# Modulation weights in stacked partition groups with selector sums, and rotary scores from stacked high and low parts

## The chip, the cores and the metric

One core of one Trainium2 chip runs the whole kernel. The metric is device time in microseconds of one execution: the kernel before takes 1735.68 us, the median of 3 runs (1734.07 to 1736.79).

## The reference

Two blocks follow each other, all in float32, for 256 tokens of width 2048. The first has two layers of latent attention, a gated short convolution and attention over a memory; the second has a Fourier mixer and a squared-ReLU MLP, both modulated by a vector `c`. What the change touches is this:

```python
# first block, for each of 2 layers l: 8 heads, 128 plain + 64 rotary dimensions
q = (rmsnorm(q_lat, q_norm_g[l]) @ w_uq[l]).reshape(b, s, 8, 192)
q = concat([q[..., :128], apply_rope(q[..., 128:], cos, sin)], axis=-1)
k_pe = apply_rope(k_pe, cos, sin)                     # one rotary key for all heads
k = concat([k_nope, broadcast_to(k_pe, (b, s, 8, 64))], axis=-1)
sc = einsum('bqhd,bkhd->bhqk', q, k) * 192 ** -0.5    # then softmax, then @ v
# second block: w_mod is 2048 x 12288 (100.7 MB), c one vector of 2048
sh1, sc1, g1, sh2, sc2, g2 = split(silu(c) @ w_mod + b_mod, 6)
h = rms_norm(x, norm_g[0]) * (1 + sc1) + sh1
x = x + g1 * rms_norm(fourier_mix(h) @ fnet_w_out, norm_g[1])
h = rms_norm(x, norm_g[2]) * (1 + sc2) + sh2
x = x + g2 * rms_norm(square(relu(h @ w_mlp_in)) @ w_mlp_out, norm_g[3])
```

## The kernel before, in words

**Steps.** The work of TensorE is cut into 576 steps, each of which multiplies half a weight unit (a unit is up to 128 x 2048 float32, 1 MB, in a ring of four, `raw`). Steps 0 to 143 are layer 0 and steps 144 to 287 layer 1 of the first block, 288 to 319 the projection of the Fourier mixer, 320 to 575 the MLP. Every weight product is made of three rounded products. ScalarE copies a half unit to its rounded high part (`split_hi`, L373 to L380) three steps ahead, VectorE subtracts for the low part (`split_lo`, L382 to L387), and TensorE multiplies high by high, high by low and low by high (`fm_half`, L398 to L409, with the weights stationary and 256 tokens moving; `tm_half`, L411 to L423, with up to 512 weight columns moving). The rounded type is `float32r`. A product of plain `float32` operands is issued as two instructions on TensorE.

**Order.** Each engine walks through the steps in a loop of its own, and at given steps does other work in its own queue's order: what stands behind a waiting instruction waits too. SyncE issues nearly all loads (L474 to L563): unit `u` when the unit four before it has been multiplied, and behind it `load_mods` (L477 to L485).

**w_mod.** The product with `silu(c)` is done on VectorE beside all the rest. The 12288 columns are taken in 12 chunks of 1024 columns. A unit is 128 rows of a chunk (512 KB, one DMA, a ring of three, `modw`), 16 units to a chunk, 192 in all; VectorE adds unit times a column of factors `cv` to `modacc` (`mod_unit`, L986 to L999, inside the step loop at L1185 and before the step's group end). `mod_plan` (L172 to L184) gives each unit a step: one of `mod_slots`, which leaves out the steps in `HEAVY`. After the 16th unit of a chunk it picks a step, at least two later, at which TensorE sums `modacc` over the partitions (`mod_sums`, L1352 to L1357: eight plain float32 products of a 128 x 128 piece of `modacc` with one column of ones into bank `M[3]`); the next chunk starts after it. TensorE waits in its order for all units of the chunk. VectorE adds the result to `modT` one step later (`mod_added`, L1001 to L1007). The sums stand at steps 49, 82, 105, 126, 166, 204, 232, 255, 277, 308, 359 and 421.

**Rotary part.** The groups `uq` (steps 40 to 47 of a layer, two steps and two heads a group) and `ukv` (steps 48 to 55) alternate between two accumulators, so a group needs the one that the group before the last used. At the end of a `uq` group ScalarE makes the half-swapped copy `swap` and the copy to `O` (L692 to L697), and VectorE makes `qpe` (L1053 to L1060). `rotary_keys` (L1086 to L1099) makes the rotated key in two zero-padded versions `kpe`, for even and odd heads. At steps 59, 62, ... 80 TensorE makes the scores of a head (L1435 to L1443): for each 128 queries one plain float32 product with `kn` and one with `kpe`.

Of the kernel before, what the change touches and what calls it, by code (L numbers as in the profile page):

```python
# [5 lines left out]
F32 = mybir.dt.float32  # L6
# [7 lines left out]
P = 128  # L14
# [124 lines left out]
MCH = MODCOLS // 1024  # L139
# [4 lines left out]
HEAVY = ({21, 24, 26, 28, 30, 31, 32, 33, 39, 40, 41, 42, 44, 46, 48, 49, 51, 52, 54, 55, 56, 63} | set(range(64, 69)) | {72, 77, 84}  # L144
# [26 lines left out]

def mod_plan():  # L172

    units, sums, free = {}, {}, -1
    for step in mod_slots():
        if len(units) == MCH * KT or step <= free:
            continue
        units[step] = len(units)
        if len(units) % KT == 0:
            free = step + 2  # L180
            while not may_sum(free):
                free += 1
            sums[free] = len(units) // KT - 1
    return units, sums  # L184
# [3 lines left out]
assert len(MOD_AT) == MCH * KT and len(MOD_SUM) == MCH  # L188
# [3 lines left out]
assert MOD_END[5] < LH + GATE_ROW[0] and MOD_END[9] < BY_TOKEN[1]  # L192
# [16 lines left out]
def build_program(nc, x, memt, positions, small, w_in, w_uq, w_ukv, w_mk, w_mv, w_o, post_g,  # L209
# [3 lines left out]
    with ctx:  # L213
# [37 lines left out]
        kpe = at("kpe", [P, 2, SEQ], A + 40)  # L251
# [30 lines left out]
        ones = at("ones", [P, 8], m + 0.5)  # L282
        gs = at("gs", [P, G_CONST], m + 0.5625)
# [16 lines left out]
        assert origin + (m + 2.34375) * 1024 <= nc.sbuf_top  # L300
# [27 lines left out]
        lat = [{n: sem(f"{w}_{n}") for n in LN} for w in ("q", "kv")]  # L328
        kpe_T, swap_in, rope_prod, rope_out, conv_step = map(sem, ("kpe_T", "swap_in", "rope_prod", "rope_out", "conv_step"))
# [11 lines left out]
        x2_xn, x2_T, x2_val, x2_hi, x2_lo = map(sem, ("x2_xn", "x2_T", "x2_val", "x2_hi", "x2_lo"))  # L341
        first_hi, first_lo, mem_first = sem("first_hi"), sem("first_lo"), sem("mem_first")
# [223 lines left out]
        def _(pool):  # L566
# [4 lines left out]
            nc.gpsimd.memset(sc[:, XP:XP + 8], EPS).then_inc(pow_set, 1)  # L571
            pool.wait_ge(pow_set, 4)
# [33 lines left out]
        def _(act):  # L606
# [65 lines left out]

            def ended(act, l, g):
# [18 lines left out]
                if name == "uq":  # L692
                    act.wait_ge(rope_out, l * 5 + i + 1)
# [4 lines left out]
                if name == "ukv":  # L698
                    nc.scalar.activation(V[:, :, 256 * i:256 * i + 256],
# [39 lines left out]
            for l in range(DEPTH):  # L739
                base = l * LH  # L740
                for s in range(LH):
# [183 lines left out]
        def _(dve):  # L925
# [60 lines left out]
            def mod_unit(at_step):  # L986

                j = MOD_AT[at_step]
                c, k = j // KT, j % KT
                dve.wait_ge(mod_in[j % MRING], 16 * (j // MRING + 1))  # L990
                co = cv[:, 2 * KT + k:2 * KT + k + 1]
                if k == 0:
# [8 lines left out]
            def mod_added(at_step):  # L1001

                if at_step - 1 in MOD_SUM:
                    c = MOD_SUM[at_step - 1]
                    dve.wait_ge(mod_T, c + 1)
                    cols = modT[:, 8 * c:8 * c + 8]
                    tt(cols, M[3][:, MODCOL:MODCOL + 8], cols, ALU.add).then_inc(mod_out, 1)  # L1007
# [78 lines left out]
            def rotary_keys(l):  # L1086

                dve.wait_ge(swap_in, 5 * l + 1)
                for e in range(2):
                    half = slice(64 * e, 64 * e + 64)  # L1090
                    nc.vector.memset(kpe[64 - 64 * e:128 - 64 * e, e, :], 0.0)
                    tt(kpe[half, e, :], M[0][half, 0:SEQ], cosT[half, :], ALU.mult)
                tt(swap[:, :], swap[:, :], sinT[:, :], ALU.mult).then_inc(rope_prod, 1)
                dve.wait_ge(rope_prod, 5 * l + 1)
                for e in range(2):
                    half = slice(64 * e, 64 * e + 64)
                    w = tt(kpe[half, e, :], kpe[half, e, :], swap[half, :], ALU.add)
                w.then_inc(rope_out, 1)
                dve.wait_ge(rope_out, 5 * l + 1)  # L1099

            for l in range(DEPTH):
                base = l * LH
                for s in range(LH):
# [100 lines left out]
                    if l == DEPTH - 1 and s == GATE_ROW[0]:  # L1204

                        dve.wait_ge(mod_out, 6)
# [46 lines left out]
            dve.wait_ge(mod_out, 10)  # L1253
# [31 lines left out]
            for q in range(4):  # L1285
                base = ML_H + 64 * q
                for s in range(65 if q < 3 else 64):
# [8 lines left out]
                    if q == 2 and s == 2:  # L1296
                        dve.wait_ge(mod_out, 12)
# [45 lines left out]
        def _(pe):  # L1343
# [8 lines left out]
            def mod_sums(at_step):  # L1352
                c = MOD_SUM[at_step]
                pe.wait_ge(mod_used, KT * (c + 1))
                for t in range(8):
                    i = mm(M[3][:, MODCOL + t:MODCOL + t + 1], modacc[:, t * P:(t + 1) * P], ones[:, 0:1], True, True)
                i.then_inc(mod_T, 1)  # L1357

            for l in range(DEPTH):
                base = l * LH  # L1360
                for s in range(LH if l + 1 < DEPTH else LH - 8):
# [60 lines left out]
                    for h in range(NH):  # L1422
# [3 lines left out]
                        if s == QK_AT[h]:  # L1426
                            if h == 0:
                                pe.wait_ge(acc_act, act_reads(l, G_OF["xin"] - 1))
                                pe.wait_ge(rope_out, l * 5 + 5)
# [151 lines left out]
            pe.wait_ge(mod_out, 10)  # L1581
# [98 lines left out]
```

## Time and profile before

| What | Value |
|---|---|
| median of 3 runs | 1735.68 us |
| the profiled execution, its own time | 1735.06 us |
| its span, first to last instruction | 1733.3 us |
| mean granted TensorE clock | 0.992 |
| TensorE busy / VectorE / ScalarE | 98% / 67% / 48% |
| bytes loaded from HBM | 404.58 MB |

Durations below come from the one profiled execution. PE is TensorE's matmuls, PEld its weight loads, DVE is VectorE, ACT ScalarE, SPq the queue of SyncE. Instructions overlap on an engine, so what one costs in a row of its like is the distance between two starts.

### The profile page before, as it was taken

How to read it: one execution, taken by the hardware profiler on the slowest of the kernel's cores; microseconds unless marked ns; L12 is line 12 of the kernel's file. 1: busy time of each engine (PE TensorE's matmuls, PEld its weight loads, DVE VectorE, ACT ScalarE, POOL GpSimd, SP SyncE). 2: the span in 40 equal slices, each digit the busy share in tenths (PEclk: the TensorE clock that was granted, in tenths of full speed). 3: DMA queues.
4: the chain of work that ended last, by engine and by line, in shares of the span. 5: the costliest groups of instructions: out<-in, count | busy, mean ns of one | idle time of the engine just before them, and what ended most of it. 6: DMA issues, size and time to landing. Idle time of an engine off the chain costs nothing.

```text
span 1733.3 us, 24590 instructions
## 1 busy us (share of the span) xinstructions
PE 1703.2 (98%) x10180; PEld 1522.9 (88%) x10180; DVE 1163.2 (67%) x1234; ACT 840.2 (48%) x1151; POOL 19.4 (1%) x34
## 2 busy tenths in 40 slices
PE   7999999999999999999999989999999999999997
PEld 7899999987889999998898878888888888888886
DVE  6777657787867767678759568776555465555555
ACT  6557445444645645544454364434443344334442
POOL 0000000000100000000000000000000000000000
PEclk9999999999999999999999989999999999999999
DMA  8688567897768857688738548788656565655663
GB/s 298 214 280 304 191 215 243 318 343 287 254 203 275 295 176 266 219 313 311 262 135 317 200 155 280 259 290 286 191 174 193 193 193 185 216 188 188 195 193 123
DMA packets 184943, 408.29 MB, mean 236 GB/s; under 512 B 8928, under 2 KB 21504, under 8 KB 184064
## 3 DMA queue, kind: packets, MB, share of 16 engines
q1 hardware_dynamic: 184336, 404.58, 68.3%
q8 instruction: 81, 1.33, 0.3%
q10 hardware_dynamic: 496, 2.14, 0.3%
q14 instruction: 30, 0.25, 0.1%
HBM read 404.58 MB, written 2.11 MB: 235 GB/s over the span
## 4 chain that ended last, share of the span: by engine, by line
PE 94%; DMA 2%; DVE 1%; issue 1%; ACT 1%; POOL 0%; DVEq 0%; SPq 0%; POOLq 0%; ACTq 0%
PE banks L390 93%; DMA modw<-in_w_mod 1%; DMA raw<-in_w_mv 1%; PE banks L1419 1%; PE banks L1382 0%; DVE modacc L998 0%; DVE wlo L386 0%; ACT whi L379 0%; DMA raw<-in_w_mk 0%; PE banks L1390 0%; DVE X L967 0%; PE banks L1575 0%; DVE xn L1179 0%; DVE otok L927 0%; ACT junk L615 0%
## 5 line engine op out<-in xcount | busy, mean ns | idle before, releaser
L386 DVE TENSOR_TENSOR wlo<-raw,whi 128x1024 fp32r<-128x1024 f32 (+3 forms) x563 | 666.4, 1189 | 449.1 <-ACT whi L379 447.7
L379 ACT ACTIVATE whi<-raw 128x1024 fp32r<-128x1024 f32 (+3 forms) x563 | 577.4, 1031 | 685.8 <-PE banks L390 657.2
L390 PE MATMUL banks<-H,whi 128*128 128x256 f32 (+1 forms) x3072 | 743.6, 325 | 1.2 <-DVE H L927 1.2
L390 PE MATMUL banks<-H,wlo 128*128 128x256 f32 x2048 | 578.1, 282 | 0.0
L390 PEld LDWEIGHTS banks<-H,whi 128*128 128x128 f32 x3072 | 515.4, 191 | 50.7 <-DVE H L927 1.6
L390 PE MATMUL banks<-whi,Y 128*128 128x512 f32 x1472 | 458.9, 391 | 1.1 <-DVE wlo L386 1.1
L390 PEld LDWEIGHTS banks<-H,wlo 128*128 128x128 f32 x2048 | 390.9, 191 | 0.1
L390 PEld LDWEIGHTS banks<-whi,Y 128*128 128x128 f32 x1472 | 277.9, 189 | 60.0 <-DVE wlo L386 1.9
L390 PE MATMUL banks<-wlo,Y 128*128 128x512 f32 x768 | 300.0, 391 | 0.0
L998 DVE SCALAR_TENSOR_TENSOR modacc<-modw,cv,modacc 128x1024 f32<-128x1024 f32 x180 | 230.1, 1279 | 17.1 <-DMA modw<-in_w_mod 17.0
L390 PEld LDWEIGHTS banks<-wlo,Y 128*128 128x128 f32 x768 | 144.9, 189 | 29.8
L390 PE MATMUL banks<-whi,H 128*128 128x512 f32 (+1 forms) x480 | 139.3, 370 | 0.0
L390 PEld LDWEIGHTS banks<-whi,H 128*128 128x128 f32 x480 | 87.7, 188 | 13.7
L390 PE MATMUL banks<-wlo,H 128*128 128x512 f32 (+1 forms) x256 | 94.5, 369 | 0.0
L390 PEld LDWEIGHTS banks<-wlo,H 128*128 128x128 f32 x256 | 48.1, 188 | 7.3
L779 ACT ACTIVATE prob<-banks,sc 128x256 f32<-128x256 f32 x48 | 22.4, 471 | 49.2 <-DVE sc L1139 49.2
L390 PE MATMUL banks<-memh,whi 128*128 128x256 f32 x128 | 38.8, 303 | 6.7 <-DVE wlo L927 6.7
L911 ACT ACTIVATE Y<-sqr 128x1024 fp32r<-128x1024 f32 x16 | 17.0, 1061 | 44.3 <-DVE sqr L1308 44.3
L390 PE MATMUL banks<-meml,whi 128*128 128x256 f32 x128 | 37.9, 296 | 0.0
L390 PE MATMUL banks<-memh,wlo 128*128 128x256 f32 x128 | 37.8, 296 | 0.0
L390 PEld LDWEIGHTS banks<-memh,whi 128*128 128x128 f32 x128 | 26.4, 206 | 7.2 <-issue 7.1
L828 ACT ACTIVATE prob<-prob,sc 128x256 f32<-128x256 f32 x48 | 21.8, 502 | 22.4 <-DVE sc L1143 22.1
(198 smaller groups left out, 1293.4 us busy)
## 6 DMA issues: line engine op xcount, KB each, us to landing
modw<-in_w_mod SPq DMA_DIRECT2D x192, 512.0 KB, 6.4
raw<-in_w_in SPq DMA_DIRECT2D x72, 1024.0 KB, 5.2
raw<-in_w_mlp_in SPq DMA_DIRECT2D x64, 1024.0 KB, 5.3
raw<-in_w_mlp_out SPq DMA_DIRECT2D x64, 1024.0 KB, 5.1
raw<-in_w_o SPq DMA_DIRECT2D x32, 1024.0 KB, 6.2
raw<-in_w_fnet SPq DMA_DIRECT2D x16, 1024.0 KB, 6.4
raw<-in_w_mv SPq DMA_DIRECT2D x8, 1024.0 KB, 6.1
raw<-in_w_mk SPq DMA_DIRECT2D x7, 1024.0 KB, 6.0
```

The lines of the kernel that those rows point to most:

```text
L379: nc.scalar.activation(hi_part(step, n), raw[u % RAW][:, (step % 2) * n:(step % 2) * n + n], ACT.Copy).then_inc(hi_ready, 1)
L386: nc.vector.tensor_tensor(wlo[u % RAW][:, part], raw[u % RAW][:, part], hi_part(step, n).bitcast(F32), ALU.subtract).then_inc(lo_ready, 1)
L390: return nc.tensor.matmul(o, a, b, start=start, stop=stop, skip_group_check=True)
L779: w = nc.scalar.activation(prob[:, b, t, :], M[b][:, t * SEQ:(t + 1) * SEQ], ACT.Exp, scale=scale, bias=sc[:, NM + 2 * b + t:NM + 2 * b + ...
L828: w = nc.scalar.activation(prob[:, b, t, :], prob[:, b, t, :], ACT.Copy, scale=sc[:, RINV + 2 * b + t:RINV + 2 * b + t + 1])
L911: nc.scalar.activation(Yhi[:, 4 * j:4 * j + 4, :], sqr[:, :, :], ACT.Copy).then_inc(m_hi, 1)
L998: nc.vector.scalar_tensor_tensor(modacc[:, :], modw[j % MRING][:, :], co, modacc[:, :], ALU.mult, ALU.add).then_inc(mod_used, 1)
L1419: i = nc.tensor.transpose(M[2][:, kt * SEQ + t * P:kt * SEQ + (t + 1) * P], prob[:, b, t, kt * P:(kt + 1) * P], ident[:, :])
```

## The change

The chunks become four passes of 64, 32, 64 and 32 units. A unit is still 512 KB in one ring slot, but its partitions are four groups of 32 (or two of 64), and each group holds the same 32 (64) rows of `w_mod` for another 1024 columns; it is loaded by four (two) DMAs. Column factors come from `cvx`, in which ScalarE repeats `cv` by groups with 20 small copies at steps 15 to 17. The sum is made of eight products with four (two) selector columns `sel`, which GpSimd sets at the start. By the planner's own rules the four sums stand at steps 125, 204, 307 and 421. Five more steps of a layer are kept free of units, and the steps freed of sums take units, so that 73, 72, 17 and 30 units stand in the two layers, the mixer and the MLP, where it was 74, 70, 17 and 31.

The rotated queries get a high part in one half of the partitions and their low part in the other (`qr`), the rotated key, which both halves hold alike, a high part `krh` and a low part `krl`. Two float32r products replace the one plain product. The key loses its two padded versions.

```diff
-MCH = MODCOLS // 1024
+MOD_PASS = ((0, 4, 0), (2 * D, 2, 64), (3 * D, 4, 96), (5 * D, 2, 160))
+MOD_UNITS = 192
-HEAVY = ({21, ..., 63} | set(range(64, 69)) | {72, 77, 84}
+HEAVY = ({21, ..., 63} | set(range(64, 69)) | {72, 77, 84, 91, 98, 119, 126, 133}
...
@@ load_mods (SyncE)
-                        k, c = j % KT, j // KT
-                        sp.dma_start(modw[j % MRING][:, :], w_mod[k * P:(k + 1) * P, 1024 * c:1024 * (c + 1)]).then_inc(mod_in[j % MRING], 16)
+                        col, groups, j0 = MOD_PASS[pass_of(j)]
+                        n, k = P // groups, (j - j0) * (P // groups)
+                        for e in range(groups):
+                            sp.dma_start(modw[j % MRING][e * n:(e + 1) * n, :],
+                                         w_mod[k:k + n, col + 1024 * e:col + 1024 * (e + 1)]).then_inc(mod_in[j % MRING], 16)
@@ GpSimd, at the start: sel[:, 0:4] and sel[:, 4:6] get ones by groups of 32 and 64 partitions (7 memsets)
@@ ScalarE
+            def rotary_hi(l, i):
+                act.wait_ge(rope_out, l * 5 + i + 1)
+                if i == 0:
+                    nc.scalar.activation(krh[:, :], kr[:, :], ACT.Copy).then_inc(rope_hi, 1)
+                else:
+                    nc.scalar.activation(qr[0:64, 2 * i - 2, :], qpe[0:64, i - 1, :], ACT.Copy)
+                    nc.scalar.activation(qr[64:128, 2 * i - 1, :], qpe[64:128, i - 1, :], ACT.Copy).then_inc(rope_hi, 1)
+            def spread_factors(part):
+                act.wait_ge(cv_step, 3)
+                for groups, c0, es in ((4, 0, (0, 1)), (4, 0, (2, 3)), (2, 64, (0, 1)))[part:part + 1]:
+                    n = P // groups
+                    for e in es:
+                        for j in range(groups):
+                            w = nc.scalar.activation(cvx[e * n:(e + 1) * n, c0 + j:c0 + groups * KT:groups],
+                                                     cv[j * n:(j + 1) * n, 2 * KT:], ACT.Copy)
+                w.then_inc(cv_ready, 1)
...
                 if name == "uq":
-                    act.wait_ge(rope_out, l * 5 + i + 1)
+                    rotary_hi(l, i)
                     for b in range(4):
...
                 if name == "ukv":
+                    if i == 0:
+                        rotary_hi(l, 4)
...
+                    if l == 0 and 15 <= s < 18:
+                        spread_factors(s - 15)
@@ VectorE
+                if j == 0:
+                    dve.wait_ge(cv_ready, 3)
...
+            def rotary_lo(l, i):
+                dve.wait_ge(rope_hi, l * 5 + i + 1)
+                if i == 0:
+                    w = tt(krl[:, :], kr[:, :], krh[:, :].bitcast(F32), ALU.subtract)
+                else:
+                    tt(qr[64:128, 2 * i - 2, :], qpe[0:64, i - 1, :], qr[0:64, 2 * i - 2, :].bitcast(F32), ALU.subtract)
+                    w = tt(qr[0:64, 2 * i - 1, :], qpe[64:128, i - 1, :], qr[64:128, 2 * i - 1, :].bitcast(F32), ALU.subtract)
+                w.then_inc(rope_lo, 1)
             def ended(l, g):
+                if name == "ukv" and i == 0:
+                    rotary_lo(l, 4)
...
                 if name == "uq":
+                    rotary_lo(l, i)
                     dve.wait_ge(swap_in, 5 * l + i + 2)
@@ rotary_keys (VectorE): two memsets and four products of 64 partitions become two of 128
@@ TensorE
-                pe.wait_ge(mod_used, KT * (c + 1))
+                groups = MOD_PASS[c][1]
+                pe.wait_ge(mod_used, MOD_LAST[c])
+                own = sel[:, 0:4] if groups == 4 else sel[:, 4:6]
                 for t in range(8):
-                    i = mm(M[3][:, MODCOL + t:MODCOL + t + 1], modacc[:, t * P:(t + 1) * P], ones[:, 0:1], True, True)
+                    i = mm(M[3][:, MODCOL + groups * t:MODCOL + groups * (t + 1)], modacc[:, t * P:(t + 1) * P], own, True, True)
...
                                     mm(o, O[:, h, tok], kn[:, h, :], True, False)
-                                    i = mm(o, qpe[:, h // 2, tok], kpe[:, h % 2, :], False, True)
+                                    mm(o, qr[:, h, tok], krh[:, :], False, False)
+                                    i = mm(o, qr[:, h, tok], krl[:, :], False, True)
```

## Rows read from the trace of the kernel before

**Rows 1.** The page: busy time of the bounding engine, and the slices.
```profile
PE 1703.2 (98%) x10180; PEld 1522.9 (88%) x10180; DVE 1163.2 (67%) x1234; ACT 840.2 (48%) x1151; POOL 19.4 (1%) x34
...
PE   7999999999999999999999989999999999999997
```

**Rows 2.** The page: shares of the chain that ended last, by line.
```profile
PE banks L390 93%; DMA modw<-in_w_mod 1%; DMA raw<-in_w_mv 1%; PE banks L1419 1%; PE banks L1382 0%; DVE modacc L998 0%; DVE wlo L386 0%; ACT whi L379 0%; DMA raw<-in_w_mk 0%; PE banks L1390 0%; DVE X L967 0%; PE banks L1575 0%; DVE xn L1179 0%; DVE otok L927 0%; ACT junk L615 0%
```

**Rows 3.** Waits of TensorE: who waited for whom, us, times, longest.
```profile
PE banks L390 <- DVE modacc L998: 2.7, 2, 2.0
```

**Rows 4.** Timeline of PE around the sum at step 49: start, us, what.
```profile
143.55 0.28 PE L390 MATMUL banks<-whi,kvl 128*128 128x256 f32 x1
143.76 1.92 PE L390 MATMUL banks<-ones,modacc 128*128 128x1 f32 x16
...
145.74 0.28 PE L390 MATMUL banks<-kvl,whi 128*128 128x256 f32 x1
```

**Rows 5.** Timeline of PE around the scores of head 0, layer 0.
```profile
164.21 0.28 PE L390 MATMUL banks<-H,wlo 128*128 128x256 f32 x1
164.33 0.60 PE L390 MATMUL banks<-kn,O 128*128 128x256 f32 x2
164.77 0.59 PE L390 MATMUL banks<-kpe,qpe 128*128 128x256 f32 x2
...
166.30 0.28 PE L390 MATMUL banks<-H,wlo 128*128 128x256 f32 x1
```

**Rows 6.** Timeline of DVE in the uq groups of layer 1.
```profile
570.07 0.43 DVE L927 TENSOR_TENSOR qpe<-banks,cosT 128x256 f32<-128x256 f32 x1
...
574.18 0.42 DVE L927 TENSOR_TENSOR qpe<-banks,cosT 128x256 f32<-128x256 f32 x1 [0.37 <-ACT swap L695]
...
578.50 0.42 DVE L927 TENSOR_TENSOR qpe<-banks,cosT 128x256 f32<-128x256 f32 x1 [0.58 <-ACT swap L695]
```

**Rows 7.** Timeline of PE where the second ukv group of layer 1 starts.
```profile
578.70 0.28 PE L390 MATMUL banks<-whi,kvl 128*128 128x256 f32 x1
579.07 0.38 PE L390 MATMUL banks<-kvh,whi 128*128 128x256 f32 x1
```

**Rows 8.** Timeline of ACT at the end of the fourth uq group, layer 1.
```profile
576.86 1.54 ACT L695 ACTIVATE swap<-banks 32x256 f32<-32x256 f32 x4
578.42 0.60 ACT L697 ACTIVATE O<-banks 128x512 f32<-128x512 f32 x1
```

**Rows 9.** Groups by shape: VectorE's operation on 64 partitions.
```profile
L927 DVE TENSOR_TENSOR kpe<-kpe,swap 64x256 f32<-64x256 f32 x4 | 1.7, 420 | 0.1
```

**Rows 10.** Two stretches after waits of TensorE: busy, granted clock, DMA share, GB/s.
```profile
394.00:402.00 8.00, 8.00 (x28) 6.79 (x29) 1.81 (x3) 0.41 (x1) 0.00 (x0) 0.57 0.47 184
784.00:792.00 8.00, 8.00 (x48) 7.53 (x49) 3.06 (x5) 2.81 (x3) 0.00 (x0) 0.79 0.23 51
```

**Rows 11.** Stretches of 40 us, VectorE's work on w_mod alone (x is units), clock, DMA share.
```profile
360.00:400.00 40.00, 12.80 (x10) 0.93 0.95 345
...
800.00:840.00 40.00, 15.56 (x13) 1.00 1.00 380
...
920.00:960.00 40.00, 16.39 (x13) 1.00 0.97 351
```

**Rows 12.** The tile modw: DMA issues on SyncE's queue, waits of VectorE (us, times), landing.
```profile
L485 SPq DMA_DIRECT2D modw<-in_w_mod x192: 327/482/1634, 63.7 to 1200.8; - x192
...
  DMA modw<-in_w_mod: 17.0, 15
...
DMA to landing us min/median/max: 4.0/6.4/10.9
```

**Rows 13.** Timeline of ACT at steps 16 and 17 of layer 0.
```profile
63.38 1.06 ACT L379 ACTIVATE whi<-raw 128x1024 fp32r<-128x1024 f32 x1 [1.42 <-PE banks L390]
...
66.58 1.06 ACT L379 ACTIVATE whi<-raw 128x1024 fp32r<-128x1024 f32 x1 [0.25 <-PE banks L390]
```

**Rows 14.** The tile ones: ScalarE's copy of 8 elements a partition, ns min/median/max.
```profile
L651 ACT ACTIVATE junk<-ones x1: 208/208/208, 2.6 to 2.6; 128x8 bf16<-128x8 f32 x1
```

More of the change, by code:

```diff
@@ L169, in may_sum, with pass_of, mod_arrived @@
     return 37 <= (step - ML_H) % 64 <= 44
+MOD_LAST = [p[2] for p in MOD_PASS[1:]] + [MOD_UNITS]
+def pass_of(j):
+    return max(c for c, p in enumerate(MOD_PASS) if p[2] <= j)
+def mod_arrived(j):
+    return sum(16 * MOD_PASS[pass_of(i)][1] for i in range(j % MRING, j + 1, MRING))
 def mod_plan():
@@ L175, in mod_plan @@
     for step in mod_slots():
-        if len(units) == MCH * KT or step <= free:
+        if len(units) == MOD_UNITS or step <= free:
             continue
         units[step] = len(units)
-        if len(units) % KT == 0:
+        if len(units) in MOD_LAST:
             free = step + 2
@@ L182, in mod_plan @@
                 free += 1
-            sums[free] = len(units) // KT - 1
+            sums[free] = MOD_LAST.index(len(units))
     return units, sums
 MOD_AT, MOD_SUM = mod_plan()
-assert len(MOD_AT) == MCH * KT and len(MOD_SUM) == MCH
+assert len(MOD_AT) == MOD_UNITS and len(MOD_SUM) == len(MOD_PASS)
 MOD_END = {c: step for step, c in MOD_SUM.items()}
 GATE_ROW = (114, 116, 118, 121)
-assert MOD_END[5] < LH + GATE_ROW[0] and MOD_END[9] < BY_TOKEN[1]
+assert MOD_END[1] < LH + GATE_ROW[0] and MOD_END[2] < BY_TOKEN[1]
 PI = 3.1415925
@@ L250, in build_program @@
         swap = at("swap", [P, SEQ], A + 38)
-        kpe = at("kpe", [P, 2, SEQ], A + 40)
+        qr = at("qr", [P, HEADS, SEQ], 32, F32R)
+        krh = at("krh", [P, SEQ], A + 40, F32R)
+        krl = at("krl", [P, SEQ], A + 41, F32R)
+        kr = at("kr", [P, SEQ], A + 41)
         V = at("V", [P, MT, HEADS * VD], A + 42)
@@ L282, in build_program @@
         ones = at("ones", [P, 8], m + 0.5)
+        sel = at("sel", [P, 8], m + 0.53125)
         gs = at("gs", [P, G_CONST], m + 0.5625)
@@ L299, in build_program @@
         PS, PN, XP, XN = 64, 5, 80, 3
-        assert origin + (m + 2.34375) * 1024 <= nc.sbuf_top
+        cvx = at("cvx", [P, 96], m + 2.34375)
+        assert origin + (m + 2.71875) * 1024 <= nc.sbuf_top
         banks = ctx.enter_context(nc.psum_tensor("banks", [P, 8, 512], F32))
@@ L571, in _ @@
             nc.gpsimd.memset(sc[:, XP:XP + 8], EPS).then_inc(pow_set, 1)
+            nc.gpsimd.memset(sel[:, :], 0.0).then_inc(sel_set, 1)
+            pool.wait_ge(sel_set, 1)
+            for e in range(4):
+                nc.gpsimd.memset(sel[32 * e:32 * e + 32, e:e + 1], 1.0).then_inc(sel_set, 1)
+                pool.wait_ge(sel_set, e + 2)
+            for e in range(2):
+                nc.gpsimd.memset(sel[64 * e:64 * e + 64, 4 + e:5 + e], 1.0).then_inc(sel_set, 1)
+                pool.wait_ge(sel_set, e + 6)
             pool.wait_ge(pow_set, 4)
@@ L988, in mod_unit @@
                 j = MOD_AT[at_step]
[L989 to L992, printed above, removed]
+                c = pass_of(j)
+                _, groups, j0 = MOD_PASS[c]
+                dve.wait_ge(mod_in[j % MRING], mod_arrived(j))
+                co = (0 if groups == 4 else 64) + j - j0
+                co = cvx[:, co:co + 1]
+                if j == 0:
+                    dve.wait_ge(cv_ready, 3)
+                if j == j0:
                     if c:
@@ L1004, in mod_added @@
                     c = MOD_SUM[at_step - 1]
+                    col, groups, _ = MOD_PASS[c]
                     dve.wait_ge(mod_T, c + 1)
-                    cols = modT[:, 8 * c:8 * c + 8]
-                    tt(cols, M[3][:, MODCOL:MODCOL + 8], cols, ALU.add).then_inc(mod_out, 1)
+                    cols = modT[:, col // P:col // P + 8 * groups].rearrange("p (e t) -> p e t", e=groups)
+                    tt(cols, M[3][:, MODCOL:MODCOL + 8 * groups].rearrange("p (t e) -> p e t", e=groups), cols, ALU.add).then_inc(mod_out, 1)
             def mod_step(at_step):
@@ L1088, in rotary_keys @@
                 dve.wait_ge(swap_in, 5 * l + 1)
[L1089 to L1092, printed above, removed]
+                tt(kr[:, :], M[0][:, 0:SEQ], cosT[:, :], ALU.mult)
                 tt(swap[:, :], swap[:, :], sinT[:, :], ALU.mult).then_inc(rope_prod, 1)
                 dve.wait_ge(rope_prod, 5 * l + 1)
[L1095 to L1098, printed above, removed]
+                tt(kr[:, :], kr[:, :], swap[:, :], ALU.add).then_inc(rope_out, 1)
                 dve.wait_ge(rope_out, 5 * l + 1)
@@ L1579, in _ @@
             by_token(1, acc[1], (Hhi, Hlo))
-            pe.wait_ge(mod_out, 10)
+            pe.wait_ge(mod_out, 3)
             pe.wait_ge(acc_dve, DVE0 + 3)
```

13 lines of the change are left out of this document (8 added, 5 removed).

## The prediction

> **What bounds the kernel.** I read the page first: TensorE is busy in 98% of the span and in every slice [rows 1], and 93% of the chain that ended last is its own matmul line [rows 2]. So time taken off TensorE's queue comes off the kernel, unless what is behind it is nearly as late. For that I read its waits: it waited for w_mod's accumulation only twice, 2.7 us in all, 2.0 us at most [rows 3]. Then the stretches: in three windows of 40 us, around 360, 800 and 920 us, the DMA engines are busy in 95 to 100% while they carry 10 to 13 units of w_mod [rows 11]. There DMA has nothing left, and TensorE keeps going only just. The kernel is bound by TensorE, with three stretches where the loads are a second bound. Last, the clock: after the two waits it is granted 0.57 over 8 us and 0.79 over 8 us, a mixture of 2.4 and 1.2 GHz [rows 10].
>
> **Fewer sums.** Twelve become four. From the last product before the sum at step 49 to the second product after it 2.19 us pass (143.55 to 145.74), where two distances of 0.12 us would stand, since 16 instructions are put between them [rows 4]. A sum costs 1.95 us, eight fewer give **-15.6 us**. A selector with four columns instead of one: the row shows one column; the instructions are spaced 0.12 us (1.95 over 16), as far apart as those with 256 moving columns [rows 4, 5], so four columns cost the same.
>
> **Rotary scores.** From one product before the scores to its like after them there are 2.09 us (164.21 to 166.30), where three distances of 0.12 us would be. The four plain products (each two instructions) so cost 1.73 us, 0.433 us each [rows 5]. Two float32r products with 256 columns cost 0.24 us in place of 0.433 us. 2 layers x 8 heads x 2 halves x 0.193 us is **-6.2 us**.
>
> **The uq groups.** Here the cover is thin. In layer 1 TensorE's second ukv group starts at 579.07 where it could at 578.82; it waits for the accumulator of the fourth uq group [rows 7], which ScalarE leaves at 579.02 [rows 8] and VectorE at 578.92 [rows 6]. The change puts one subtraction ahead of the first group's rotation and two ahead of each later one; VectorE's operation on 64 partitions takes 0.42 us [rows 9], and I take 0.4 us apart. VectorE then runs late: 0.4 us after the first group; 1.2 after the second, which had no idle time; 1.2 + 0.8 - 0.37 = 1.63 after the third; 1.63 + 0.8 - 0.58 = 1.85 after the fourth [rows 6]. Its product with `cosT`, the last reader, ends at 578.92 + 1.85 = 580.8 us, so the ukv group starts 1.7 us later. ScalarE, with two more copies, would let go at 579.8 and isn't last [rows 8]. In layer 0 the sum at step 49 covered the 0.25 us of before; it is gone, so 2.0 us there. Together **+3.7 us**, between 0 (if the two engines catch up) and 8 us (ScalarE's copies and VectorE's subtractions in full, one after the other: 1.6 us more a group, less the idle). What is queued behind VectorE's new waits for ScalarE (`rope_hi`) is its next `split_lo`, made three steps ahead, so that wait itself costs nothing.
>
> **Costed at nothing, and by what cover.** The 20 copies that spread the factors: no row has this shape; the nearest are 0.21 us (8 elements a partition [rows 14]) and 0.38 us (a quarter of the 1.54 us for four with 32 partitions [rows 8]). At steps 15 and 16 eight of them are 1.7 to 3.0 us each time, where ScalarE had 1.42 us of idle time a step and then 0.25 us [rows 13]. It runs some 2 us late behind a lead of three steps of about 3.2 us (63.38 to 66.58 is one). If that cover failed, the start of the projection would slip by 2 us. The GpSimd memsets and the waits on `sel` and `cvx` lie tens of us ahead of their first use. The key's rotation saves VectorE four operations a layer, in a place where nobody waits.
>
> **The loads.** A unit is issued as four or two DMAs. One issue takes 0.33 us at least and 0.48 us in the middle [rows 12]; I take 0.35 us for each of a chain, so the last part of a unit lands 1.05 us later. Two units in a pair of steps make eight issues, 2.8 us, and the weight unit's own, in 5.4 to 5.8 us of TensorE's time: SyncE holds. Landing takes 6.4 us in the middle and up to 10.9 us [rows 12], with a ring of three and two steps' lead, so in the three full stretches some of this shows. Lower end 0, upper end 1.05 us at each of the four sums and some at three or four places where VectorE waits, 8 us; I take **+2 us**, nearer the lower end, because VectorE waited for a unit 15 times as it is [rows 12] and only two of these reached TensorE [rows 3].
>
> **The two waits at sums.** They cost 2.7 us [rows 3], and the clock after them 8 x 0.43 + 8 x 0.21 = 5.1 us of work [rows 10]. They belong to the sums at 126 and 255 (393.5 and 783.6 us). The second is gone, the first comes at 125 with two units fewer just ahead of it. Between -7.8 us and 0; I take half, **-3.9 us**.
>
> Against the profiled execution's own 1735.1 us: -15.6 - 6.2 + 3.7 + 2 - 3.9 = -20.0, so 1715.1 us. That execution lies 0.6 us under the median, which is nothing here: **1715 us**, 1708 to 1721 within this case.
>
> **Rival 1, slower: the parts of a unit load at half the rate.** No DMA of the trace fills only 32 or 64 partitions of a tile with rows of this size, so the price of that is open. If the 16 engines hinder one another when they all write into a quarter or half of the partitions, a unit's 512 KB, which at 390 GB/s (about the rate of the full stretch [rows 11] shows, 380) take 1.3 us, take up to 2.6. The windows then need 38 + 13, 40 + 17 and 38.8 + 17 us of DMA time in 40, an excess of 11 + 17 + 16 = 44 us, which comes out as waits of TensorE, since weights and units share the queue. That gives 1715 + 45 = **1760 us**; windows next to these would add to it. At half the price it is 21 us, and 1736. It decides from about 0.6 us a unit. Against it: the bytes, the row length of 4 KB and the number of rows are unchanged, only their order and their partitions are new. The Trainium skill ("SBUF — State Buffer", Door 1: The DMA port swizzle) says that partitions 0 to 31, and 0 to 63 as well, reach only 8 of the 16 DMA-side ports and so get half the bandwidth, and that two transfers to different halves don't add up. By that rule the doubled price would hold in full; no row here shows or refutes it. I give this case 28%: no row bears the price out, but the windows leave no room for it if it is there.
>
> **Rival 2, faster by half: TensorE runs into the loads.** Bytes are the same in less time. Of the eight sums that go, those at 105, 255 and 277 stand just ahead of a full stretch or just behind it. If the loads bound there, 3 x 1.95 = 5.9 us are given back and the waits stay (3.9 us): **1725 us**. For it speaks the DMA share of 0.95 to 1.00 [rows 11], against it that TensorE waited for w_mod at two sums alone [rows 3]. 15%.
>
> **Rival 3, no change**: half of rival 1's price, or a uq stage that costs more together with rival 2: around 1736 us, 7%.
>
> **How the numbers follow.** Forecast 50%, rival 2 15%, rival 1 28%, rival 3 7%. A measurement of this kernel can tell 0.2% (3.5 us) from no change: faster 65%, within it 7%, slower 28%. The range for 8 in 10 reaches from 1708, the lower end of the forecast, to 1762, just past rival 1's middle.
>
> **What would show it.** The row of `banks<-ones,modacc` becomes `sel`, with 64 instructions and not 192; `kpe` goes, and 128 instructions on `qr` take 15 us instead of 19 busy, spaced 0.12. In the uq groups of both layers TensorE waits 1.7 to 2 us for VectorE or ScalarE at step 50. DMA to landing of `modw` stays near 6.4 us (7 to 8), its issues are 640. If landing rises to 9 us and more and the DMA share at 360, 800 and 920 us stays at 1.00 while TensorE waits for `modacc` or `wlo`, rival 1 holds, and a lower granted clock will stand behind each wait. If TensorE's waits at sums grow though landing doesn't, the forecast's last two terms are wrong.

## The result, and the profile after

The changed kernel takes **1809.45 us** (median of 4 runs, 1801.59 to 1821.73) against 1735.74 us before (4 runs): the ratio is 1.0445, with a 95% interval of 1.0415 to 1.0474. It is 74 us slower; 1715 was forecast, and rival 1 gave 1760.

The page of the kernel after: TensorE's busy time, the slices of TensorE, of its clock and of the DMA engines, the loads' queue, and the chain that ended last.

```profile
span 1806.3 us, 24824 instructions
...
PE 1714.4 (95%) x10052; PEld 1519.5 (84%) x10052; DVE 1166.3 (65%) x1236; ACT 843.7 (47%) x1189; POOL 22.2 (1%) x41
...
PE   7999999979999899998899789999999999999997
...
PEclk9999999999999999998999889999999999999999
DMA  8799897999879968899956848999655655655553
...
q1 hardware_dynamic: 191504, 404.61, 77.6%
...
PE 70%; DMA 19%; DVE 5%; issue 2%; SPq 2%; ACT 1%; POOL 0%; DVEq 0%; POOLq 0%; ACTq 0%
```

Before, TensorE was busy for 90% or more of every slice but the first, the 24th and the last [rows 1]; now six slices from the ninth to the 24th fall below that, and the clock falls in three of them. It held 93% of the chain by its matmul line alone [rows 2]; now all of it holds 70%, and DMA 19%. TensorE still bounds most of the kernel, but in a fifth of the chain the bound has gone to the loads. The same 404.6 MB keep the 16 DMA engines busy for 77.6% of 1806.3 us, 1401.7 us.

Who waited for whom in the kernel after (us, times, longest), first TensorE, then VectorE and ScalarE, then SyncE's queue:

```profile
PE banks L416 <- DVE wlo L412: 47.0, 29, 3.6
...
PE banks L416 <- DVE modacc L1063: 3.2, 1, 3.2
PE banks L416 <- ACT O L754: 3.1, 2, 1.6
...
DVE modacc L1063 <- DMA modw<-in_w_mod: 166.1, 63, 8.3
...
ACT whi L405 <- DMA raw<-in_w_o: 116.4, 22, 8.5
...
ACT whi L405 <- DMA raw<-in_w_mlp_out: 54.9, 14, 6.7
...
SPq L513 <- DVE modacc L1063: 158.3, 73, 9.0
```

VectorE waited 17.0 us for w_mod before [rows 12]; now 166. What holds TensorE most is `wlo`, the low part of a weight tile, for which it waits 29 times: VectorE makes `wlo` as well as the products with w_mod, and ScalarE waits for `raw` ahead of it. The sums are the smaller part, but more than the one row of 3.2 us: TensorE also idles 3.65 us ahead of the second sum and 2.30 us ahead of the third, where the view names no engine ("issue"). VectorE's timeline does, here at the second sum:

```profile
634.45 1.28 DVE L1063 SCALAR_TENSOR_TENSOR modacc<-modw,cvx,modacc 128x1024 f32<-128x1024 f32 x1 [4.15 <-DMA modw<-in_w_mod]
```
```profile
635.83 2.23 PE L416 MATMUL banks<-sel,modacc 128*128 128x2 f32 x16 [3.65 <-issue]
```

The pass's last product ends at 635.73 and the sum starts 0.10 us later; at the third sum it is 1024.70 and 1024.81. So three of the four sums wait, 9.1 us in all, where two of twelve waited 2.7 us before [rows 3].

The landing time of a piece of w_mod shows less than the waits do: 6.4 us in the middle before [rows 12], 6.5 now, but of pieces a quarter or half the size, and up to 17.4. The tile `modw` after (issues on SyncE's queue, the start of the first and last product, landing):

```profile
L513 SPq DMA_DIRECT2D modw<-in_w_mod x640: 310/422/2846, 63.5 to 1264.3; - x160
L1063 DVE SCALAR_TENSOR_TENSOR modacc<-modw,cvx,modacc x188: 1264/1281/1287, 79.6 to 1277.7; 128x1024 f32<-128x1024 f32 x188
...
DMA to landing us min/median/max: 2.5/6.5/17.4
```

The loop that binds stands in the timelines. First VectorE, then SyncE's queue, then TensorE, from 374 to 382 us:

```profile
374.79 1.29 DVE L1063 SCALAR_TENSOR_TENSOR modacc<-modw,cvx,modacc 128x1024 f32<-128x1024 f32 x1 [1.27 <-DMA modw<-in_w_mod]
375.99 1.22 DVE L988 TENSOR_TENSOR Y<-gate,Y 128x1024 fp32r<-128x1024 f32 x1
377.13 1.22 DVE L412 TENSOR_TENSOR wlo<-raw,whi 128x1024 fp32r<-128x1024 f32 x1
```
```profile
376.11 1.70 SPq L513 DMA_DIRECT2D modw<-in_w_mod  x4
377.85 0.42 SPq L379 DMA_DIRECT2D raw<-in_w_o  x1
```
```profile
376.70 0.39 PE L416 MATMUL banks<-whi,Y 128*128 128x512 f32 x1
378.49 0.47 PE L416 MATMUL banks<-whi,Y 128*128 128x512 f32 x1 [1.41 <-DVE wlo L412]
```

The product with w_mod waits for its unit; `wlo`, queued behind it on VectorE, comes late, and TensorE idles 1.41 us. The product ends at 376.08 (374.79 + 1.29), and only then is the ring's slot free and SyncE can issue the next unit's four DMAs (376.11); the next weight tile is issued behind them, at 377.85. A late unit makes the next unit and the next weight tile late too.

Two stretches of 40 us and one of 8 us (busy time of each engine, granted clock, DMA share, GB/s):

```profile
360.00:400.00 40.00, 31.89 (x126) 24.39 (x125) 27.54 (x25) 15.06 (x18) 0.00 (x0) 0.95 1.00 253
...
800.00:840.00 40.00, 32.86 (x206) 29.44 (x204) 23.78 (x21) 14.12 (x14) 0.00 (x0) 0.91 1.05 285
...
408.00:416.00 8.00, 7.84 (x29) 6.88 (x30) 2.36 (x3) 1.06 (x1) 0.00 (x0) 0.57 0.63 183
```

At a share of 0.95 to 1.05 the DMA engines moved 345 and 380 GB/s before [rows 11] and move 253 and 285 now. Busy is not moving: each piece takes longer. The clock of 0.57 behind the sum at step 125 is what stood behind the sum at 126 [rows 10]: that wait was not avoided.

### The profile page after: what moved, and what is told of

It is laid out like the page before. It is cut to its first block, busy times and chain, and to the rows that moved or that the text cites. A ratio compares the mean times of both kernels' runs of the same rounds, so it can differ in the third digit from the quotient of the medians.

```text
span 1806.3 us, 24824 instructions
## 1 busy us (share of the span) xinstructions
PE 1714.4 (95%) x10052; PEld 1519.5 (84%) x10052; DVE 1166.3 (65%) x1236; ACT 843.7 (47%) x1189; POOL 22.2 (1%) x41
## 3 DMA queue, kind: packets, MB, share of 16 engines
q1 hardware_dynamic: 191504, 404.61, 77.6%
## 4 chain that ended last, share of the span: by engine, by line
PE 70%; DMA 19%; DVE 5%; issue 2%; SPq 2%; ACT 1%; POOL 0%; DVEq 0%; POOLq 0%; ACTq 0%
PE banks L416 69%; DMA modw<-in_w_mod 17%; DVE modacc L1063 3%; SPq L513 2%; DVE wlo L412 1%; DMA raw<-in_w_mlp_out 1%; DMA raw<-in_w_mv 1%; ACT whi L405 1%; PE banks L1495 1%; PE banks L1458 0%; SPq L379 0%; DMA raw<-in_w_mk 0%; DVE otok L988 0%; DVE X L1028 0%; PE banks L1652 0%
## 5 line engine op out<-in xcount | busy, mean ns | idle before, releaser
L405 ACT ACTIVATE whi<-raw 128x1024 fp32r<-128x1024 f32 (+3 forms) x563 | 569.0, 1029 | 737.3 <-PE banks L416 428.6
L416 PE MATMUL banks<-whi,Y 128*128 128x512 f32 x1472 | 472.3, 399 | 31.5 <-DVE wlo L412 31.4
L416 PEld LDWEIGHTS banks<-whi,Y 128*128 128x128 f32 x1472 | 284.0, 193 | 99.3 <-issue 31.9
L1063 DVE SCALAR_TENSOR_TENSOR modacc<-modw,cvx,modacc 128x1024 f32<-128x1024 f32 x188 | 240.7, 1280 | 166.5 <-DMA modw<-in_w_mod 166.1
L416 PE MATMUL banks<-wlo,Y 128*128 128x512 f32 x768 | 305.1, 397 | 0.0
L416 PE MATMUL banks<-whi,H 128*128 128x512 f32 (+1 forms) x480 | 144.0, 379 | 7.8 <-DVE wlo L412 7.8
L614 POOL TENSOR_TENSOR sc<-sc 128x1 f32<-128x1 f32 (+1 forms) x18 | 13.5, 750 | 1593.7 <-DVE sc L1408 729.5
```

Of the source, the lines that this page charges most:

```text
L405: nc.scalar.activation(hi_part(step, n), raw[u % RAW][:, (step % 2) * n:(step % 2) * n + n], ACT.Copy).then_inc(hi_ready, 1)
L416: return nc.tensor.matmul(o, a, b, start=start, stop=stop, skip_group_check=True)
L614: nc.gpsimd.tensor_tensor(sc[:, r0:r0 + n], sc[:, m0:m0 + n], sc[:, POW:POW + n], ALU.pow).then_inc(done, 1)
L1063: nc.vector.scalar_tensor_tensor(modacc[:, :], modw[j % MRING][:, :], co, modacc[:, :], ALU.mult, ALU.add).then_inc(mod_used, 1)
```

## The experiments

### Is it the partitions that a DMA reaches, or the number of DMAs?

**The kernel before, each unit by four DMAs of 32 partitions.**

```diff
-sp.dma_start(modw[...][:, :], w_mod[k * P:(k + 1) * P, 1024 * c:1024 * (c + 1)])
+for e in range(4):
+    sp.dma_start(modw[...][32 * e:32 * e + 32, :],
+                 w_mod[k * P + 32 * e:k * P + 32 * e + 32, 1024 * c:1024 * (c + 1)])
```

(VectorE's wait counts all four DMAs; likewise in the next kernel.)

> The kernel before, with one edit: each unit of w_mod is loaded by four DMAs of 32 partitions and 4 KB rows in place of one of 128 partitions. Rows, columns, sums, slots and the rotary part stay as before. Theory 1 (a DMA that fills only 32 or 64 partitions moves at about half the rate): the share of the 16 engines' time goes from 68% to about 77%, and the time to 1790 to 1830 us, since the sums aren't saved here. Theory 2 (the number of issues and completions, 768 in place of 192, holds SyncE and the ring up): the same slowdown, but DMA share stays near 68 to 70%. Theory 3 (the new plan of slots or the four column blocks of the source are to blame): within 5 us of the kernel before.

Measured: **1847.06 us**, ratio 1.0662 (1.0621 to 1.0702). The loads' queue and TensorE's waits:

```profile
q1 hardware_dynamic: 193552, 404.61, 76.7%
...
PE banks L390 <- DVE wlo L386: 37.7, 21, 6.2
PE banks L390 <- DVE modacc L1000: 36.3, 6, 12.8
```

The engines' share is the 77% expected for half-rate DMAs; the time lies above the 1790 to 1830 us. This one edit, with none of the change's passes, selectors or rotary copies, loses 113 us, more than the whole change does. It has twelve sums, and TensorE waits at them six times.

**The kernel before, each unit by four DMAs of all 128 partitions**, 256 columns each.

```diff
+for e in range(4):
+    sp.dma_start(modw[...][:, 256 * e:256 * e + 256],
+                 w_mod[k * P:(k + 1) * P, 1024 * c + 256 * e:1024 * c + 256 * e + 256])
```

> The kernel before, with one edit: each unit of w_mod is loaded by four DMAs of all 128 partitions and 256 columns (1 KB rows) each. As many issues and completions as in the run with four DMAs of 32 partitions, but each fills all partitions. Theory 1 (partitions): a few per cent more DMA time for the shorter rows, so 1736 to 1750 us. Theory 2 (issues): 1780 us or more, as with 32 partitions. Theory 3: as the kernel before.

Measured: **1740.59 us**, ratio 1.0047 (1.0029 to 1.0065).

```profile
q1 hardware_dynamic: 267280, 404.61, 71.1%
...
DVE modacc L1000 <- DMA modw<-in_w_mod: 27.1, 22, 3.8
```

As many issues (768) as in the kernel above, and rows a quarter as long; it loses about 6 us to the unchanged kernel of its own batch (1734.41; 5 to 11 us by the interval), and the other 113. So the number of DMAs isn't it.

**The loads alone.** Nine ways of filling a buffer with 4 MB, one after the other, nothing beside them; nothing of the reference is computed. Here `n` is the number of partitions, and `step` takes every step-th of them.

```diff
+dst = buf[p0:p0 + (n - 1) * step + 1:step, c0:c0 + nb * 1024].rearrange("p (k n) -> p k n", n=1024)
```

> Loads alone, nothing computed: the output is whatever the last loads left, so its time says nothing of the task. Nine forms of 4 MB each, one after the other, all with 4 KB rows but for one: eight DMAs of 512 KB to 128 partitions; to partitions 0 to 31; to 0 to 63; to a quarter of the partitions in turn; to halves in turn; to every fourth partition (32 of them, spread over all); 32 DMAs of 128 KB to quarters in turn; 32 of 128 KB to all partitions with 1 KB rows; and halves from two queues at once. Theory 1 as a matter of how many partitions a DMA fills in one block: about 10 to 11 us for 128 partitions and 20 us for each form of 32 or 64, also in turn, since each of the 16 engines takes its DMAs in order. If the quarters in turn take 10 us, the change's loss isn't there. Open is whether every fourth partition, and two queues, run at 10, at 15 or at 20 us; I expect 20 for the first and 15 to 20 for the second.

Stretches of 4 us inside each form (granted clock, DMA share, GB/s): all 128 partitions; partitions 0 to 31; 0 to 63; the four quarters in turn; the two halves in turn; every fourth partition, starting at 0, 1, 2, 3 in turn. The last three rows: 128 KB in 4 KB rows to the quarters in turn, which is the piece that the change loads; 128 KB in 1 KB rows to all 128; the two halves from two queues at once.

```profile
4.00:8.00 4.00, 0.00 (x0) 1.00 1.03 421
...
20.00:24.00 4.00, 0.00 (x0) 1.00 1.03 206
...
44.00:48.00 4.00, 0.00 (x0) 1.00 1.03 207
...
68.00:72.00 4.00, 0.00 (x0) 1.00 1.01 213
...
88.00:92.00 4.00, 0.00 (x0) 1.00 1.03 221
...
108.00:112.00 4.00, 0.00 (x0) 1.00 0.98 359
...
124.00:128.00 4.00, 0.00 (x0) 1.00 1.04 235
...
144.00:148.00 4.00, 0.00 (x0) 1.00 0.87 265
...
164.00:168.00 4.00, 0.00 (x0) 1.00 1.03 289
```

A block of 32 or of 64 partitions gets about half the rate, whichever block comes next. Here the Trainium skill ("SBUF — State Buffer", Door 1: The DMA port swizzle), which the prediction weighed, agrees with the rows: 32 and 64 alike, at half. What was not expected is every fourth partition: 32 partitions again, but 359 GB/s. It isn't the number of partitions that counts but where they lie. The same section's table of ports has these 32 partitions on all 16 ports. That two transfers to different halves don't add up, which the prediction took along, holds only in part here: from one queue the halves ran at 221 GB/s, but from two queues at once at 247 to 289 in the windows from 160 to 172 us, against 207 for one half. Every kernel here loads w_mod from one queue.

### The change with its loads put right

**Whole units.** The whole change, but w_mod is laid out unit by unit before the launch, and each unit is one DMA to 128 partitions.

```diff
-for e in range(groups):
-    sp.dma_start(modw[j % MRING][e * n:(e + 1) * n, :],
-                 w_mod[k:k + n, col + 1024 * e:col + 1024 * (e + 1)])
+sp.dma_start(modw[j % MRING][:, :], w_mod[j])
```

> The whole change, but w_mod is laid out unit by unit before the launch (the same numbers in another order), so that a unit with its four or two partition groups is one DMA of 128 partitions and 4 KB rows. Plan, selectors, sums and rotary part are those of the change. Theory 1 (partitions per DMA): the slowdown goes, and with it what the prediction summed comes out, 1710 to 1720 us, DMA share near 68%. Theory 3 (plan, selectors or the rotary chain are to blame): 1790 us or more still.

Measured: **1711.34 us**, ratio 0.9863 (0.9848 to 0.9878), faster than both. Its page and its waits:

```profile
PE 1678.4 (98%) x10052; PEld 1500.6 (88%) x10052; DVE 1169.6 (68%) x1236; ACT 851.4 (50%) x1189; POOL 20.9 (1%) x41
...
q1 hardware_dynamic: 184336, 404.58, 69.0%
...
PE banks L416 <- ACT O L751: 3.1, 2, 1.6
...
DVE modacc L1060 <- DMA modw<-in_w_mod: 15.4, 15, 3.1
```

Its span is 1708.6 us. Against it the change's loads keep the DMA engines busy 1401.7 - 1178.9 = 223 us longer, 1.16 us for each of 192 units. TensorE idles 91.9 us instead of 30.2, and is busy 36.0 us longer for the same 10052 instructions. Most of that is the clock: granted 0.978 in the mean against 0.995, it gave 0.022 x 1806.3 - 0.005 x 1708.6 = 31 us less of full speed (an estimate). 61.7 + 36.0 is the whole difference of the spans, 97.7 us.

**The kernel before with units laid out ahead** (w_mod reordered into consecutive 512 KB, one DMA a unit, all else as before) is the control for the new order in memory.

> The kernel before, with w_mod laid out unit by unit before the launch, one DMA of 128 partitions to a unit as before. It tells whether the gain of the version with whole units comes from the order of the source. Theory (order doesn't matter): 1731 to 1737 us, the 6.2 us of landing unchanged. Rival (512 KB in one piece load faster): 1725 us or less, with landing under 5.5 us.

Measured: 1731.87 us, ratio 0.9987 (0.9973 to 1.0001). The order of the source is worth nothing that can be told from zero.

**Woven groups.** Group e goes to partitions e, e + 4, e + 8, ... (or e, e + 2, ...). Source, order and number of DMAs (640) are those of the change; factors and selectors follow the new placement, the factors loaded already spread.

```diff
-sp.dma_start(modw[j % MRING][e * n:(e + 1) * n, :],
+sp.dma_start(modw[j % MRING][e:P:groups, :],
```

> The change with its units' partition groups woven into each other: group e lies in partitions e, e+4, e+8, ... (e, e+2, ... where there are two), so that each of the unit's four or two DMAs reaches over all 128 partitions; as many DMAs (640), the same rows of w_mod, the same order, the same three passes, selectors and four sums. The factors are loaded already spread, and the selectors are summed out of the identity; the rest is the change. My theory (a unit's DMAs, each within a block of 32 or 64 partitions, run at about half rate, 206 against 421 GB/s in the run of the loads alone, and that makes 80 or more of the 98 us between the change and the kernel with whole units): every fourth partition ran at 325 to 359 GB/s there, so a unit's 512 KB should need about 1.5 us instead of 2.5 us against 1.25 us; the loads are then short by some 40 us in the full windows at most instead of the whole, most of it hidden: 1715 to 1740 us, likeliest 1722, the vector engine's waits for modw at 20 to 60 us instead of 166, none of over 5 us in the tensor engine for the eviction of wlo. Rival (the number of DMAs, 640 instead of 192, each with its issue and its completion, is what costs): nothing changes, 1790 to 1820 us. Rival (the order in which w_mod is read): nothing changes either.

Measured: **1715.63 us**, ratio 0.9909 (0.988 to 0.9938).

```profile
q1 hardware_dynamic: 191504, 404.65, 69.3%
...
DVE modacc L1040 <- DMA modw<-in_w_mod: 22.5, 20, 3.5
...
360.00:400.00 40.00, 40.00 (x186) 33.40 (x185) 29.88 (x29) 17.24 (x23) 0.00 (x0) 1.00 0.93 328
```

This is the decisive run: the same pieces on other partitions take 94 of the 98 us away. It also drops the 20 copies of the factors and the memsets, but the kernel with whole units has these and is as fast, so they aren't the cause. What is left to the kernel with whole units, 1715.63 against 1709.93 on the same chip, is 5.7 us for four or two DMAs a unit instead of one. SyncE's queue has less room: an issue takes 0.59 us in the middle instead of 0.50, there are 640 and not 192, and the queue waits only 32.0 us for a free slot of the ring, not 95.6. The third sum waits 1.87 us for its last unit. The issues and the lower rate of such a DMA (359 against 421 GB/s) were not told apart.

### The parts

**Rotary alone**, on the kernel before (the copies, the stacked products, and the keys' rotation).

> The kernel before with the rotary part of the change alone. By the prediction's terms: 6.2 us saved in the scores, 1.7 us given back at the second ukv group of layer 1; in layer 0 the sum at step 49 still stands and covers 0.25 us, so 1.7 us there too: 1735.7 - 6.2 + 3.4 = 1733 us. Rival: VectorE and ScalarE catch up and 1730 us come out; or each uq group waits and it is 1737 us or more.

Measured: 1731.61 us, ratio 0.9979 (0.9966 to 0.9992), which of 1734.41 us is -3.6 us, between -5.9 and -1.4. The sum of terms gave -2.8. It expected 1.7 us of waiting in each layer; TensorE waited 1.5 us for `O` in layer 1, and in layer 0 1.1 us for `modacc` at the sum of step 49, whose last product VectorE had behind its rotary work.

**Whole units without rotary.**

> The version with whole units without the rotary part: passes, selectors and four sums alone. By the prediction's terms 15.6 us for the sums and up to 7.8 us for the two waits at sums and the clock behind them: 1713 to 1720 us. If it is above 1725 us, the sums were not worth what the rows said, and the rotary part is worth more than it showed by itself.

Measured: 1713.34 us, ratio 0.9888 (0.9862 to 0.9913). Against the control on the same chip (1731.87), the passes and four sums instead of twelve bring -18.5 us; no sum waits any more, where 3.1 us were waited in the control. In the profiles the rotary part then takes TensorE's busy time from 1685.1 to 1678.4 us and gives 3.1 us back as the two waits for `O`. In the kernel with whole units, the timeline of VectorE in the last uq group of layer 1, then that of TensorE:

```profile
567.24 0.85 DVE L985 TENSOR_TENSOR qr<-qpe,qr 64x256 fp32r<-64x256 f32 x2
568.13 0.42 DVE L985 TENSOR_TENSOR qpe<-banks,cosT 128x256 f32<-128x256 f32 x1
```
```profile
566.82 0.28 PE L416 MATMUL banks<-whi,kvl 128*128 128x256 f32 x1
568.65 0.35 PE L416 MATMUL banks<-kvh,whi 128*128 128x256 f32 x1 [1.56 <-ACT O L751]
```

The row names ScalarE's copy of `O`, but by ScalarE's timeline that had ended at 567.81; the accumulator is free when the product with `cosT` ends, at 568.55. The two subtractions into `qr` stand ahead of it.

**Copies moved.** Whole units, the high parts behind the copy of `O`, the low parts behind the rotation. The kernel with whole units was run again beside it as the measure.

```diff
 if name == "uq":
-    rotary_hi(l, i)
     (swap, O)
+    rotary_hi(l, i)
 ...
-    rotary_lo(l, i)
     (rotation)
+    rotary_lo(l, i)
```

> The kernel with whole units, with the rotary copies moved: the high parts on the scalar engine behind its copy of the key group's scores (O) instead of ahead of it, the low parts on the vector engine behind the rotation of the next group. My theory (the tensor engine waits 1.6 us for O before the second ukv group in each layer, because the low part that the vector engine writes waits for the high part's copy and the rotation of the next group stands behind it): the chain is shorter by up to a copy and a subtraction, 0.4 us each, in each group, and the wait shrinks by 0.8 to 1.6 us in each layer: 1708 to 1710.5 us against 1711.3. Rival (the wait hangs on the product of w_mod that the vector engine does at step 47, of which this changes nothing): same time within 0.5 us, the wait still 1.4 to 1.6 us.

> The kernel with whole units once more, beside the two with moved copies on the same chip: 1709.5 to 1713 us, as before (1711.34). It is the measure for the two: a difference under 1 us between them and this one isn't told apart.

Measured: 1708.57 us (1707.82 to 1710.9) against 1709.93 us (1709.54 to 1710.9), so -1.4 us, with ranges that overlap. The wait in the kernel with the copies moved:

```profile
PE banks L416 <- ACT O L751: 1.8, 2, 0.9
```

It shrank from 3.1 us in all, by 0.65 us a layer where 0.8 to 1.6 were expected. The times are too near to say more.

**Copies moved, and step 47 without a unit** (47 added to `HEAVY`; the sums move to 126, 205, 308 and 421).

> As the kernel with the moved copies, and step 47 (the uq groups' step of layer 1) takes no unit of w_mod; the unit goes to a later step, and the sums to steps 126, 205, 308 and 421. My theory: with both, the tensor engine's wait for O before the second ukv group is gone in layer 1: 1707 to 1710 us. Rival (the moved unit falls on a step that has no time to spare): a new wait of 1 to 3 us for modacc or for an eviction, 1710 to 1713 us.

Measured: 1710.3 us (1708.63 to 1710.66). The wait for `O` is gone in both layers and nothing is won, for a new wait stands at the first sum:

```profile
PE banks L416 <- DVE modacc L1061: 1.5, 1, 1.5
```

The rival with the new wait for `modacc` held, as far as ranges that overlap with the 1708.57 can tell.

**One DMA a unit from the layout as it is.** Woven groups as one DMA, with the copies moved. The lines are set against those of the kernel with woven groups.

```diff
-for e in range(groups):
-    sp.dma_start(modw[j % MRING][e:P:groups, :],
-                 w_mod[k:k + n, col + 1024 * e:col + 1024 * (e + 1)])
+sp.dma_start(modw[j % MRING][:, :],
+             w_mod[k:k + n, col:col + 1024 * groups].rearrange("n (e f) -> n e f", e=groups))
```

> The kernel with woven groups, but each unit as one DMA instead of four or two: the source is the 32 (64) rows of 4096 (2048) columns, read in its own order, so that each row's four (two) pieces of 1024 columns fall on four (two) neighbouring partitions, all 128 in turn; no array is reordered before the launch. And the rotary copies stand where the kernel with moved copies has them. My theory (it is the partitions that one DMA reaches that set its rate, and the DMAs' number counts for little): as the kernel with whole units and moved copies, which took 1708.57 us: 1707 to 1712 us, the loads' share of the engines 68.5 to 69.5%, no wait of the tensor engine for modacc. Rival (the cut source makes the DMA slow, as the blocks did): over 1720 us, with vector engine waits for modw over 30 us.

Measured: **1708.66 us** (1708.45 to 1709.38), ratio 0.9853 (0.9831 to 0.9876), with nothing of w_mod reordered before the launch (only the vector `c` is laid out by groups). It is as fast as the kernel with whole units and moved copies, 1708.57.

```profile
q1 hardware_dynamic: 184336, 404.62, 68.8%
...
DVE modacc L1040 <- DMA modw<-in_w_mod: 11.4, 11, 2.8
```

TensorE doesn't wait for `modacc` in it. It beats both kernels: 25 us under before, 101 under the change as it was made.

## Why the prediction was wrong

**The step that failed first** is the choice of the likeliest case. "Against it: the bytes, the row length of 4 KB and the number of rows are unchanged, only their order and their partitions are new": the last word of that sentence is the cause. The rows of before held no DMA to part of the partitions, so they said nothing either way, and I let silence count as evidence for no cost. The two ends of that unknown were 0 and 1.3 us a unit; 1.16 us were measured, and the Trainium skill ("SBUF — State Buffer", Door 1: The DMA port swizzle) stood at that end; I held it at 28% because no row bore it out. The sign I named for it would have misled me too: landing was to rise from 6.4 to 9 us and more, and it stayed at 6.5 us in the middle, because a landing is now that of a piece and not of a unit. The waits for `wlo` and the GB/s at a full share told it.

**The step that failed second** is rival 1's own price, 44 us counted in three full windows ("windows next to these would add to it", and they were left at nothing). The starts of the four sums in the change and in the kernel with whole units show where the loss arose:

| | sum 1 | sum 2 | sum 3 | sum 4 | end |
|---|---|---|---|---|---|
| whole units, us | 383.4 | 590.2 | 937.5 | 1268.3 | 1708.6 |
| the change, us | 408.2 | 635.8 | 1024.8 | 1366.0 | 1806.3 |
| lost in the stage, us | 24.8 | 20.8 | 41.7 | 10.4 | 0 |

The 360 us window was priced at 11, and its stage lost 24.8. The second stage has none of my windows and lost 20.8. The third and fourth together were priced at 33 and lost 52.1. The sum by windows lets each stretch spread its DMA work freely over 40 us. The kernel can't: with a ring of three a unit's issue waits for the product of the third one before it, and the weight tile stands behind it in SyncE's queue. That this is why partly filled windows lost too was not tried by itself (a deeper ring would do it); the chain supports it, with DMA on `modw` at 17% of it. And the price was counted in time of the loads alone, while 36 of the 98 us are TensorE's longer busy time, most of it the clock behind the waits. I had named that as a sign to look for and put no number to it.

**The other terms**, each by its own test:
- Fewer sums -15.6 and the two waits -3.9, together -19.5: measured -18.5. Right together, where units arrive in time; no run parts the two. In the change itself three of four sums waited, 9.1 us.
- Rotary -6.2: half a head's three products take 0.67 us instead of 0.87 (2 x 0.433 [rows 5]), and TensorE's busy time fell by 6.7. Right, though the sign for it was miscounted: 64 instructions on `qr` and not 128, 23.9 us busy and not 15. The uq groups +3.7, with TensorE waiting 1.7 to 2 us a layer: 3.1 us, 1.6 at most in each layer, with VectorE last as said. Together -2.5: measured -3.6 (-5.9 to -1.4).
- The issues of 640 DMAs +2, of at most 8: 5.7 us between woven groups and whole units. Mis-sized but inside its bounds: an issue took 0.42 us in the middle in the change and 0.59 with woven groups, where I had 0.35.
- The spread factors and the memsets at nothing: no wait names them in the kernel with whole units, where a copy takes 0.23 us in the middle.

So the forecast's case came out at 1715.63 us in the kernel with woven groups, whose arithmetic and number of loads are the change's. The sum was right for a kernel that was not the one made, and that it hits so nearly is in part luck: that kernel lies 17.9 us under its own before (1733.55), where 20.0 were summed.

Rival 2 (TensorE runs into the loads where they bind) is refuted: with whole units TensorE was busy for all 40 us of the stretches at 360 and 800 us.

## What to carry to other kernels

When a tile is filled by several DMAs, ask which partitions each one reaches. Here a block of 32 or 64 loaded at about half rate, even where the blocks together make 128. Woven through the partitions (e, e + 4, e + 8, ...) the same groups load at 359 of 421 GB/s, and as one DMA whose source rows are cut into pieces for neighbouring partitions they cost nothing. Where before has no row for a new form of transfer, its price is open at both ends, and silence is no evidence for the cheap one. Where the DMA engines already look full, nothing hides the dear one: here each late load made the next ones late, and the clock took a further share.

## What the runs showed of the hardware

- Loads of 4 KB rows ran at 421 GB/s on all partitions, at 206 and 207 on partitions 0 to 31 and 0 to 63, at 213 on quarters in turn, and at 359 on every fourth partition. The DMA engines were busy 98 to 103% of the time in the windows shown: the share alone doesn't show a slow transfer, the GB/s beside it do.
- With 1 KB rows to all 128 partitions, 128 KB a DMA, it was 265 GB/s at a share of 0.87, and yet that form cost the kernel only 6 us: its 71.1% of 1737.5 us are 1235 us of engine time, 52 more than before's 1184 (68.3% of 1733.3 us), against the blocks' 1414. The 265 GB/s were set by the issues and not by the engines: that form's 32 DMAs were issued in 15.06 us, 0.47 us each, and 128 KB in 0.47 us are 279 GB/s (an estimate). The quarters' 235 GB/s, as quickly issued (14.98 us), came at a share of 1.04. So at nearly the same rate one form leaves the engines time and the other none.
- TensorE's product of 128x4 for a selector costs what 128x1 did (1.92 us for sixteen [rows 4]): sixteen take 1.84 us in the kernel with whole units.

```profile
383.38 1.84 PE L416 MATMUL banks<-sel,modacc 128*128 128x4 f32 x16
```
